# Layer 1's later modulation by VectorE in the dense stage, and a fourth bank for the scores of its attention

## The reference

```
for l in range(2):
    sh1, sc1, g1, sh2, sc2, g2 = split(silu(c) @ ada_w[l] + ada_b[l])       # modulation, 6 x 1024 columns
    csh1, ..., cg2             = split(silu(c_ctx) @ ada_w[l] + ada_b[l])   # the same for the context
    h  = rms(x) * norm1_w[l] * (1 + sc1) + sh1                              # and hc from ctx
    p  = h @ w_in[l]                                                        # q, k, v, retention, convolution
    x += g1 * (concat(attention(p), retention(p), convolution(p)) @ w_out[l])
    h2 = rms(x) * norm2_w[l] * (1 + sc2) + sh2
    x += g2 * (swiglu(h2) if l == 0 else mixture_of_8_experts(h2))
    # layer 0 does all of this for ctx as well; layer 1 needs only hc (keys, values, states)
```

## Time and profile before

| | us |
|---|---|
| median of 3 runs (1872.62 to 1875.18) | 1875.16 |
| profiled execution | 1873.73 |
| its span, first to last instruction | 1871.9 |

### The profile page before, as it was taken

One profiled execution on the slowest core, in us unless ns is written; L12 is line 12 of the kernel. 1 busy time (PEld: TensorE's weight loads), 2 busy tenths in 40 slices (PEclk: granted clock), 3 DMA queues, 4 the chain that ended last, 5 costly groups with the idle time before them and its releaser, 6 DMA issues.

```text
span 1871.9 us, 22029 instructions
## 1 busy us (share of the span) xinstructions
PE 1805.6 (96%) x8956; PEld 1477.5 (79%) x8956; DVE 1332.3 (71%) x1245; ACT 1049.1 (56%) x989; POOL 121.3 (6%) x128
## 2 busy tenths in 40 slices
PE   4999999999999999899999999999999999999998
PEld 2986477888888879668888888888888888888886
DVE  2478645332433358755989899999898998999998
ACT  3233843332122243464777777777777777777774
POOL 1020800000000012231000000000000000000000
PEclk9999999999999999999999999999999999999999
DMA  8325913522432133574799999999999999999994
GB/s 298 129 90 185 354 56 81 146 85 85 112 91 84 62 104 121 179 272 180 290 378 374 345 361 366 367 374 362 344 375 362 375 360 346 374 358 376 369 367 163
DMA packets 246199, 472.81 MB, mean 253 GB/s; under 512 B 10578, under 2 KB 60596, under 8 KB 246092
## 3 DMA queue, kind: packets, MB, share of 16 engines
q1 hardware_dynamic: 242000, 468.14, 70.0%
q10 hardware_dynamic: 4092, 3.20, 0.6%
HBM read 470.26 MB, written 1.05 MB: 252 GB/s over the span
## 4 chain that ended last, share of the span: by engine, by line
PE 89%; DVE 5%; ACT 2%; DMA 2%; POOL 1%; issue 1%; SPq 0%; ACTq 0%; POOLq 0%; DVEq 0%
PE bank L569 26%; PE bank L571 26%; PE bank L570 26%; DMA raw<-in_ada_w_dram 2%; PE bank L592 2%; DVE parts L1768 1%; PE bank L1142 1%; PE bank L821 1%; PE bank L810 1%; PE bank L1093 1%; PE bank L802 1%; PE bank L1105 1%; ACT parts L1332 1%; PE bank L877 1%; PE bank L753 1%
## 5 line engine op out<-in xcount | busy, mean ns | idle before, releaser
L1783 DVE TENSOR_TENSOR expert_low<-expert_loaded,expert_high 128x2048 fp32r<-128x2048 f32 x336 | 765.4, 2289 | 92.9 <-ACT expert_high L1472 92.3
L1472 ACT ACTIVATE expert_high<-expert_loaded 128x2048 fp32r<-128x2048 f32 x336 | 642.9, 1919 | 201.4 <-PE bank L571 201.4
L569 PE MATMUL bank<-expert_high,XEr 128*128 128x512 f32 x896 | 353.3, 394 | 0.7 <-DVE XEr L1783 0.7
L571 PE MATMUL bank<-expert_high,XEr 128*128 128x512 f32 x896 | 349.3, 390 | 0.0
L570 PE MATMUL bank<-expert_low,XEr 128*128 128x512 f32 x896 | 349.1, 390 | 0.0
L1332 ACT ACTIVATE parts<-raw 128x2048 fp32r<-128x2048 f32 (+1 forms) x62 | 113.2, 1831 | 271.0 <-PE bank L571 250.9
L1768 DVE TENSOR_TENSOR parts<-raw,parts 128x2048 fp32r<-128x2048 f32 (+1 forms) x62 | 135.8, 2194 | 138.5 <-ACT parts L1332 138.2
L571 PEld LDWEIGHTS bank<-expert_high,XEr 128*128 128x128 f32 x896 | 168.2, 188 | 35.5
L569 PEld LDWEIGHTS bank<-expert_high,XEr 128*128 128x128 f32 x896 | 168.3, 188 | 34.1 <-issue 0.8
L570 PEld LDWEIGHTS bank<-expert_low,XEr 128*128 128x128 f32 x896 | 168.4, 188 | 33.4
L569 PE MATMUL bank<-expert_high,HTr 128*128 128x512 f32 x448 | 174.5, 389 | 0.0
(11 more groups left out here) (248 smaller groups left out, 2266.0 us busy)
## 6 DMA issues: line engine op xcount, KB each, us to landing
expert_loaded<-in_moe_w_gate_dram SPq DMA_DIRECT2D x112, 1024.0 KB, 5.3
expert_loaded<-in_moe_w_up_dram SPq DMA_DIRECT2D x112, 1024.0 KB, 5.6
expert_loaded<-in_moe_w_down_dram SPq DMA_DIRECT2D x112, 1024.0 KB, 5.3
raw<-in_ada_w_dram SPq DMA_DIRECT2D x28, 1024.0 KB, 8.1
more<-in_ada_w_dram SPq DMA_DIRECT2D x20, 1024.0 KB, 7.6
raw<-in_w_in_dram SPq DMA_DIRECT2D x12, 1024.0 KB, 5.1
raw<-in_ffn_w_gate_dram SPq DMA_DIRECT2D x22, 512.0 KB, 4.0
raw<-in_ffn_w_up_dram SPq DMA_DIRECT2D x22, 512.0 KB, 5.3
```

The lines of the kernel that those rows point to most:

```text
L569: nc.tensor.matmul(out, st[0], mv[0], start=start, stop=False)
L571: return nc.tensor.matmul(out, st[1], mv[0], start=False, stop=stop)
L1472: nc.scalar.activation(high[:, m % PARTS, :], loaded[:, at, :], ACT.Copy).then_inc(hi_ready, 1)
L1783: return nc.vector.tensor_tensor(out, a, b, op)
```

## The change

The 16 items of group 2 leave layer 1's attention. Their `ADA_ITEMS` are zero, and there is no row copy, no fold and no wait for `rows_out` in layer 1. They are loaded in the dense stage into raw slot 3, one between two weight items (`late_item`, behind the weight item three steps on). In steps 1 to 16 VectorE adds one item a step (`add_late`): four dependent operations on 128x512 that accumulate weights times `cond`, two items (one slice) into one half of `YG`. TensorE then sums each slice over the partitions (`late_sums`): four float32 matmuls with 128 columns of `YG` as stationary and one column of ones as moving operand. The first of the eight also does the bias, four matmuls. They stand behind tiles 3, 5, 7, 9, 13, 15 and 17, and one in the first down projection. At the stage's end VectorE adds bias and sums (`late_ada_columns`). VectorE waits for the fifth sums before the first gated addition. The scores of layer 1's attention use four banks in turn.

```diff
-ADA_ITEMS = ((2, 1, 2, 1, 2, 1, 2, 1, 2, 2, 2, 2, 2, 2, 0, 0), (2, 3, 2, 3, 2, 2, 2, 0))
+ADA_ITEMS = ((2, 1, 2, 1, 2, 1, 2, 1, 2, 2, 2, 2, 2, 2, 0, 0), (0,) * 8)
+LATE_SLOT = RAW - 1
+LATE = 2 * (ADA_SLICES - EARLY)
+LATE_STEP = [1 + i if i < 10 else HALF_FF + i - 10 for i in range(LATE)]
+LATE_COLUMNS = {3: 0, 5: 1, 7: 2, 9: 3, HALF_FF + 2: 5, HALF_FF + 4: 6, HALF_FF + 6: 7}
...
+                        if f % HALF_FF >= 3 and f - 3 in LATE_STEP:
+                            late_item(LATE_STEP.index(f - 3))
...
+            def late_sums(i):
+
+                pe.wait_ge(late_used, 2 * (i + 1))
+                if i == 0:
+                    for j in range(SLICE // P):
+                        out = OB[:, P + ADA_COLS * j + 2 * EARLY:P + ADA_COLS * (j + 1)]
+                        nc.tensor.matmul(out, biasr[:, j * P:(j + 1) * P],
+                                         table("bias_same")[0:2 * ADA_SLICES, 2 * EARLY:ADA_COLS], start=True, stop=True)
+                for j in range(SLICE // P):
+                    c = ADA_COLS * j + 2 * (EARLY + i)
+                    mm = nc.tensor.matmul(OB[:, c:c + 1], YG[:, i % 2, j * P:(j + 1) * P], table("ones")[:, 0:1],
+                                          start=True, stop=True)
+                mm.then_inc(cols_full if 2 * i + 2 == LATE else late_columns, 1)
...
+                if layer:
+                    ring_v[0] = len(VB)
...
-                after(rows_out)
+                if layer == 0:
+                    after(rows_out)
...
-                                    fold_rows(layer + 1)
+                                    if layer == 0:
+                                        fold_rows(1)
...
+                        if f in LATE_COLUMNS:
+                            late_sums(LATE_COLUMNS[f])
...
+                            if p0 == 0 and half == 0 and f0 == ff_split[1][0]:
+                                late_sums(4)
...
+                if is_ada and n == ADA_FIRST[2]:
+                    sp.wait_ge(cols_full, 2)
                 if holder[s] is not None:
                     was_ada, before = holder[s]
-                    sp.wait_ge(ada_used if was_ada else lo_ready, before + 1)
+                    if was_ada and before >= ADA_FIRST[2]:
+                        sp.wait_ge(late_used, before - ADA_FIRST[2] + 1)
+                    else:
+                        sp.wait_ge(ada_used if was_ada else lo_ready, before + 1)
...
+            def add_late(step_of):
...
+                dve.wait_ge(raw_loaded[r], 16 * ada_loaded[n])
+                if half:
+                    dve.wait_ge(late_used, i)
+                else:
+                    emptied()
+                    if i >= 4:
+                        dve.wait_ge(late_columns, i // 2 - 1)
+                for j in range(KT // 2):
+                    k = half * KT // 2 + j
+                    c = cond[:, k, COND_PAD:COND_PAD + 1]
+                    if k == 0:
+                        ins = nc.vector.tensor_scalar(out, w[:, j, :], c, None, ALU.mult)
+                    else:
+                        ins = nc.vector.scalar_tensor_tensor(out, w[:, j, :], c, out, ALU.mult, ALU.add)
+                    if j < KT // 2 - 1:
+                        step(ins)
+                ins.then_inc(late_used, 1)
...
-                    if m == last:
-                        ada_rows(layer + 1)
+                    if m == last and layer == 0:
+                        ada_rows(1)
...
                             split_to(n)
+                            add_late(f)
                         hidden_low(p0 + HALF_FF - 1)
...
+                                    if p0 == 0 and half == 0:
+                                        dve.wait_ge(late_columns, 5)
```

More of the change, by code:

```diff
@@ L183, in build @@
         VB, AB, OB = bank[0:4], bank[4:7], bank[7]
-        rows_bank = (OB, VB[3], VB[3])
+        rows_bank = (OB, VB[3])
         def table(name):
@@ L304, in build @@
         ada_used = sem("modulation_weights_used")
+        late_used, late_columns = sem("late_modulation_weights_added"), sem("late_modulation_columns_made")
         distance_in = sem("distances_in")
@@ L422, in ada_items @@
             slices = ([(0, s) for s in range(EARLY)],
-                      [(0, s) for s in range(EARLY, ADA_SLICES)] + [(1, s) for s in range(EARLY)],
-                      [(1, s) for s in range(EARLY, ADA_SLICES)])[group]
+                      [(0, s) for s in range(EARLY, ADA_SLICES)] + [(1, s) for s in range(EARLY)])[group]
             n = 0
@@ L429, in ada_items, with late_item @@
                     n += 1
+        def late_item(i):
+            ada_item(1, EARLY + i // 2, i % 2, LATE_SLOT)
         for layer in range(DEPTH):
@@ L439, in build @@
                     n += 1
-            ada_items(layer + 1)
+            if layer == 0:
+                ada_items(1)
             first["out", layer] = len(items)
@@ L460, in build @@
                                         .rearrange("(k p) n -> p k n", p=P)], f1 - f0, SLICE, n % 3, n % 3)
+                            if p0 == 0 and h == 0:
+                                late_item(LATE_STEP.index(HALF_FF - 3 + ff_split.index((f0, f1))))
                             n += 1
@@ L583, in ada_product @@
                 n_h[0] += 1
-                group = 0 if n < ADA_FIRST[1] else 1 if n < ADA_FIRST[2] else 2
+                group = 0 if n < ADA_FIRST[1] else 1
                 opening, closing = n == ADA_FIRST[group], n + 1 == ADA_FIRST[group + 1]
@@ L596, in fold_rows @@
             def fold_rows(group):
-                c0, c1 = ((0, 2 * EARLY), (0, ADA_COLS), (2 * EARLY, ADA_COLS))[group]
+                c0, c1 = ((0, 2 * EARLY), (0, ADA_COLS))[group]
                 fold = table("fold")[:, c0:c1]
@@ L1249, in _ @@
                 if is_ada and s == RAW:
-                    sp.wait_ge(conv_full, CONV_OUTS * (1 if n < ADA_FIRST[2] else 2))
+                    sp.wait_ge(conv_full, CONV_OUTS)
+                if is_ada and n == ADA_FIRST[2]:
+                    sp.wait_ge(cols_full, 2)
                 if holder[s] is not None:
                     was_ada, before = holder[s]
-                    sp.wait_ge(ada_used if was_ada else lo_ready, before + 1)
+                    if was_ada and before >= ADA_FIRST[2]:
+                        sp.wait_ge(late_used, before - ADA_FIRST[2] + 1)
+                    else:
+                        sp.wait_ge(ada_used if was_ada else lo_ready, before + 1)
                 holder[s] = (is_ada, n)
@@ L1796, in ada_columns @@
             def ada_columns(group):
-                s0, s1 = ((0, EARLY), (0, ADA_SLICES), (EARLY, ADA_SLICES))[group]
+                s0, s1 = ((0, EARLY), (0, ADA_SLICES))[group]
                 after(cols_full)
@@ L1800, in ada_columns, with late_ada_columns @@
                                            OB[:, 0:96].rearrange("p (j s r) -> p j s r", s=ADA_SLICES, r=2)[:, :, s0:s1, :]))
+            def add_late(step_of):
+                if step_of not in LATE_STEP:
+                    return
+                i = LATE_STEP.index(step_of)
+                n = ADA_FIRST[2] + i
+                _, s, half, r = adas[n]
+                out, w = YG[:, (i // 2) % 2, :], ada_slot(r)
+                dve.wait_ge(raw_loaded[r], 16 * ada_loaded[n])
[15 more added lines that the diff above has]
+                ins.then_inc(late_used, 1)
+            def late_ada_columns():
+                after(cols_full)
+                out = ada[:, :, :].rearrange("p (s j) r -> p j s r", s=ADA_SLICES)[:, :, EARLY:, :]
+                bias, sums = (OB[:, a:a + 96].rearrange("p (j s r) -> p j s r", s=ADA_SLICES, r=2)[:, :, EARLY:, :] for a in (P, 0))
+                step(nc.vector.tensor_copy(out, bias))
+                step(tt(out[:, :, :, 0], out[:, :, :, 0], sums[:, :, :, 0], ALU.add))
             def vectors():
@@ L2354, in _ @@
                     mix_low(layer, t, 1)
-                ada_columns(layer + 1)
+                if layer == 0:
+                    ada_columns(1)
                 scale_columns(1, mod2_ready, layer + 1)
@@ L2402, in _ @@
                             vectors()
+                            late_ada_columns()
                             scale_columns(0, mod1_ready, 2)
```

## The result

The changed kernel takes 1876.62 us, median of 19 runs (1873.68 to 1880.55), against 1874.3 for the kernel before in the same rounds (19 runs, 1869.85 to 1878.25). The ratio is 1.0016, 95% interval 1.0009 to 1.0023: slower by 3.0 us (1.7 to 4.3); the two medians lie 2.3 us apart. That is a small slowdown, clear of the noise, where the forecast was -0.3 us, no change.

The account below looks back on a forecast made before the run. TensorE, busy 96% of the span, bounds the dense stage; in layer 1's attention GpSimd's convolution chain runs beside TensorE's. Removed 8.4 us against added 8.1 gives -0.3 us, forecast 1875.0 us, range 1869 to 1881.5.

Parts of the forecast that it names:

- The attention's gain: Layer 1's attention: scores of step 7 at 817.4 against 822.02 once modulation products and their load leave; gain 4.5 us.
- the late sums and the bias: Dense stage, TensorE: eight sums 7.0 us at 0.11 a pass, bias 1.1; 8.1 us, all on the path.
- the time outside the span: Before the first and after the last instruction: 1.8 us around the span, carried over unchanged into the forecast.
- the first rival: Layer 1's attention: without products TensorE's clock falls to half; 2 to 4 us, up to 5 + 1.7; chance 0.2.
- The step on which the forecast hung: Layer 1's attention, loop step 5: GpSimd's convolution additions limit the exponentials' start to 812.0, a gain of only 0.5 us.
- The step behind it: Layer 1's attention, exponentials of step 5 to scores of step 7: 2.16 + 3.28 us, from 812.0 to 817.4.
- The rule cited with the rival: Trainium skill on HAM oscillation: idle TensorE is throttled to half clock, paid again after every long pause; speaks against the change.
- 0.4 + 1.8 + 1.7 forecast: Layer 1's output projection: row copy gone 0.4 us, fold removed net 1.8, low clock behind the fold gone 1.7.
- VectorE and the transfers cost 0: Dense stage: an item's additions take 3.1 us with 3.4 to spare, late transfers have 7.8 us; cost 0.
- The whole return: Rival, layer 1's attention: additions run at 0.72 instead of 0.93, 6 us more return, 1869; chance 0.15 for 1857 to 1871.
- Late additions or transfers: Rival, dense stage: TensorE waits in up to 15 steps, 1 to 3 us each, 1890 us; chance 0.05.
- Nothing in the attention: Rival, layer 1's attention: no gain there, only dense cost and fold remain, +4.2 us, 1879.4; chance 0.05.

Follow-up runs that it names:

- the narrow convolution: Layer 1's convolution cut to 64 of 256 columns, in either kernel; loop 20.13 us in the changed kernel, 28.22 in the kernel before; whole times say nothing.
- the products put back: Changed kernel with three score banks and the removed float32 modulation products back in layer 1's attention, without their loads; 1880.01 us, ratio 1.0031.
- the early bias: Changed kernel with the four bias matmuls moved from before the first late sum to before the dense stage's first transposes; 1882.01 us, ratio 1.0045.
- the additions alone: Kernel before with only VectorE's late additions added in the dense stage, on a free tile, without loads and waits; 1874.66 us, ratio 1.0004.
- the sums and the bias alone: Kernel before with only the late sums' and bias matmuls added to the dense stage, on constants, read by nobody; 1881.19 us, ratio 1.004.

## Why the prediction was wrong

Three terms failed. The attention's gain was taken at full clock (4.5 us; 2.8 came, 1.7 being lost to the low clock), the late sums and the bias were priced too low (8.1 us; 8.9 measured), and the time outside the span was taken as unchanged, without a reason (it grew by 1.1 us). The sum of the forecast was so close to zero that these sizes decided.

**Attention: 4.5 forecast, 2.8 measured.** This is the term that failed most, and it failed by the first rival. The step on which the forecast hung stood: exponentials of step 5 gained 0.56 us (0.5 forecast), GpSimd's additions run in one row, and the narrow convolution shows them to be the limit. The step behind it, from 812.0 to 817.4, took 7.11 - 5.4 = 1.7 us more, because turns, values and scores ran at half clock. The narrow convolution shows 5.23 for it at full clock, and the products put back show that the clock stays up when TensorE has no pause. I gave this rival 0.2 with 2 to 4 us, up to 6.7; in the profile it cost 1.7 us, over the changed kernel's runs it may differ (mean clock 0.983 to 0.991, some 7 us between the ends, whose stages no profile shows), and in the kernel with the early bias it is 10.10 - 5.23 = 4.9. What the prediction held against it, that a pause is 1.7 us at most, was no reason: the rows show pauses of 0.57 to 1.54 us, and the clock fell. It should have had the largest chance. The Trainium skill's page "TensorE: Matmul & The Clock Gate", section "A second HAM failure mode: psum-queue depth-cycling", which I had not weighed, tells of a bf16 kernel in which frequent short idles between groups of matmuls made the clock swing between its two levels; the rows at 807.18 to 815.21 agree, and the kernel with the products back, with no such idles, stays at 1.00. The rule cited with the rival is of long pauses, and those rows have none over 1.54 us. What the rows do not explain is the length of the stretch: the early bias has it go on for 17 us without a pause.

**Output projection: 0.4 + 1.8 + 1.7 forecast, 0.7 + 1.8 + 1.6 measured.** The scores of step 7 to the projection gained 0.68. From the projection's start to the gate spread 13.81 - 10.44 = 3.37 us, of which 845.14 - 840.27 = 4.87 against 842.96 - 836.31 = 6.65 are 1.78, and the rest, 1.59, is the clock. Both come back with the fold (3.38). But putting the stretch down to the fold was too simple: with the additions alone the fold runs, the clock stays at 1.00, and from the projection's start to the gate spread it is 12.25 us, 1.6 less than in the kernel before. Seven of the profiles have the fold, six of them the low stretch, none of the ten without it (in the one with the early bias the attention's long stretch reaches to 834.8 and no new one follows). The fold helps to bring it on, and does not by itself decide.

**Dense stage: 8.1 forecast, 8.9 measured.** Each sum is 0.95 us, 8 x 0.95 = 7.6 in place of 7.0: 0.119 a pass in place of 0.11, since a pass at the row's full 0.12 was the better reading than the one with the last end taken off. The first half holds four sums and the bias: 5.29 - 0.17 = 5.12, less 3.80, leaves 1.3 for the bias, the upper end of 0.9 to 1.3. VectorE and the transfers cost 0, as forecast: the additions alone show it, and the sums and the bias alone bring 8.8 of the 8.9. In the mark at 778.33 the shift is only 7.48, because a short stretch at clock 0.50 that the kernel before has about 756, outside the change, is missing in the profile after, 1.6 us. All five profiles without sums in the dense stage have this stretch; of the nine with whole sums and the bias at its place only one has it (the narrow convolution), and the three with the bias moved or the sums cut all have it. So its absence mostly goes with the added work, although nothing near 756 was edited. Why is not shown, and the prediction had no term for it. It fits that the sums alone cost 8.8 in the dense stage of their profile, in which the stretch is missing, but 7.5 over whole runs.

**Outside the span: 1.8 forecast, 2.9 measured.** The forecast took "span and 1.8 around it" as fixed. It was 1.8 to 2.0 in every run of the kernel before and 2.8 to 3.3 in every run of the changed one and of its variants that take one expert pass. The 1.1 us are over a third of the measured 3.0. The additions on VectorE alone bring 0.7 of it; the sums and two semaphores bring nothing, 66 short copies at most 0.1. Why operations in the middle of the program lengthen what lies outside it stays open, as does the rest of some 0.4.

**The sum.** Profile against profile: 0.17 + 8.92 - 1.61 (dense stage and behind it) - 0.56 - 2.28 - 0.68 - 3.37 + 0.0 = 0.6 in the span, and 1.1 outside, 1.7 in all. Against the forecast's -0.3 the misses are 1.7 (attention), 0.8 (sums and bias) and 1.1 (outside), with 1.6 (the stretch at 756) the other way; a shift of 0.2 ahead of the dense stage and 0.2 more gain in the output projection cancel. Without the 1.6 the terms would give 3.3. The runs say 3.0 (1.7 to 4.3) and do not decide between the two. The forecast's 1875.0 us also stands on a median of three runs, 1875.16, where 19 runs have 1874.3; the ratio does not hang on that.

**The other rivals.** The whole return did not come: GpSimd's additions were not spaced closer, 30 of them from 793.63 to 823.37, 29.7 us against 30.1. Late additions or transfers did not come: VectorE kept 3.55 us to spare. "Nothing in the attention" was wrong by the gains above. No variant beats both kernels: what keeps the clock up costs more than it brings (1880.0), and what shortens the dense stage (the early bias, 1882.0) loses more to the low clock.

## What to carry to other kernels

Work that fills TensorE's pauses off the path can have a second value, its clock: before it is moved into a stage in which TensorE is full, price the stage it leaves at half speed as well (here 6.8 to 23.9 us of it, 1.7 us of loss in the profile), and count the move twice, at its new place in full and at its old place only down to the next limit. Where a second engine's chain ends within a microsecond of the one that is shortened, the gain is that microsecond: shorten either chain alone to see it. When gains and costs of 8 us each are set against each other, an error of a tenth on each decides the sign, and the time outside the span belongs in the sum.

## What the runs showed of the hardware that was not expected

- TensorE at granted clock 0.50 for 13 us and more while it was busy for 13.45 of 15 us: once low, it stayed low through some three steps, and in the kernel with the early bias through 23 us, 17 of them without a pause. At half clock the values took 3.31 in place of 1.73 us, the scores 2.01 in place of 1.06.
- Where the low stretches lie depends on more than the work beside them: two profiles of the same kernel had 13.7 and 10.2 us at 0.50 in the attention, and with four matmuls of the bias moved some 500 us ahead it was 23.9.
- 64 dependent operations of 128 x 512 on VectorE in the middle of the program lengthened the run outside the span by 0.7 us and the span by nothing that can be told.
- A float32 matmul of one column with a new 128 x 128 stationary costs 0.24 us in a full stream (0.95 for four).
